# A two-block kernel: deferred norm and piecewise first loads in the retention layer, its q, k and out products as split passes, and the recurrent layer in thirds of its channels

## What is computed

```python
def rms_norm(x, g):
    y = x * rsqrt(mean(x * x, axis=-1) + 1e-6)
    return y * g

for layer in range(2):
    h = rms_norm(x, norm_g[layer, 0])
    m = retention_mixer(h, ret_w_in, ret_w_out) if layer == 0 else rglru_mixer(h, ...)
    x = x + rms_norm(m, norm_g[layer, 1])
    f = swiglu_ffn(rms_norm(x, norm_g[layer, 2]), ffn_w_in[layer], ffn_w_out[layer])
    x = x + rms_norm(f, norm_g[layer, 3])
```

```python
y, u = split(x @ w_in)                    # y = gelu(y), u = conv4(u)
r, i = sigmoid(u's blocks @ gate_w + gate_b)
log_a = -8 * r * softplus(-a_param); a = exp(log_a)
b = sqrt(-expm1(2 * log_a)) * (i * u)
h[t] = a[t] * h[t-1] + b[t]               # every channel by itself
out = (h * y) @ w_out
```

## Time and profile before

| what | value |
|---|---|
| median of 3 runs | 1721.5 us (1720.58 to 1722.06) |
| the profiled execution's own time | 1722.84 us |
| its span, first to last instruction | 1721.0 us |
| PE busy | 1590.1 us (92% of the span) |
| DVE, ACT, POOL busy | 678.4, 519.0, 40.8 us |
| chain that ended last | PE 80%, DVE 12%, ACT 5%, waiting for nothing shown 2% |
| moved by DMA | 382.88 MB, mean 222 GB/s |

### The profile page before, as it was taken

The page is one execution under the profiler, slowest core; times in us unless marked ns, Lnnn a source line. Parts: engine busy times, 40 slices in busy tenths (PEclk is TensorE's granted clock), DMA queues, the critical chain, the costliest instruction groups (busy, mean ns, idle before and its releaser), DMA issues.

```text
span 1721.0 us, 21762 instructions
## 1 busy us (share of the span) xinstructions
PE 1590.1 (92%) x9230; PEld 1179.3 (69%) x9230; DVE 678.4 (39%) x1059; ACT 519.0 (30%) x769; POOL 40.8 (2%) x37
## 2 busy tenths in 40 slices
PE   6999999999999599999889988787899999999996
PEld 6988689999898379999734675466444444444443
DVE  3433407665574617764334536602211121111112
ACT  5430025444454425444432214322111111011111
POOL 0000001000031001000000000000000000000000
PEclk8999999999999799999899999998899999999999
DMA  9543336455644445545621220020599999999991
GB/s 404 183 169 142 135 123 243 186 196 181 247 171 185 196 170 222 184 169 188 244 72 75 98 104 1 1 83 18 209 423 425 416 425 421 422 420 423 420 422 85
DMA packets 26985, 382.88 MB, mean 222 GB/s; under 512 B 3056, under 2 KB 3184, under 8 KB 3360
## 3 DMA queue, kind: packets, MB, share of 16 engines
q1 hardware_dynamic: 26208, 377.71, 55.5%
q0 software_dynamic: 704, 4.11, 0.6%
HBM read 380.76 MB, written 1.05 MB: 222 GB/s over the span
## 4 chain that ended last, share of the span: by engine, by line
PE 80%; DVE 12%; ACT 5%; issue 2%; DMA 1%; POOL 1%; DVEq 0%; ACTq 0%; SPq 0%; POOLq 0%
PE ps L478 71%; PE ps L876 4%; PE ps L885 4%; DVE w_lo L1268 2%; DVE HM L1280 2%; ACT HM L945 2%; DVE HM L1268 2%; DVE work L1280 2%; DVE work L1268 1%; ACT work L945 1%; ACT L945 1%; DVE X L1280 1%; DMA work<-in_ctx 1%; DVE work L1274 0%; DVE in_lo L1280 0%
## 5 line engine op out<-in xcount | busy, mean ns | idle before, releaser
L478 PE MATMUL ps<-ring,work 128*64 128x512 f32 x1536 | 336.9, 594 | 12.3 <-ACT work L945 12.3
L478 PE MATMUL ps<-in_hi,w_hi 128*128 128x256 f32 x896 | 255.9, 286 | 9.9 <-DVE in_lo L1280 5.1
L1268 DVE TENSOR_TENSOR w_lo<-ring,w_hi 128x1024 fp32r<-128x1024 f32 x156 | 200.4, 1291 | 158.9 <-ACT w_hi L945 158.9
L945 ACT ACTIVATE work<-ps 128x512 f32<-128x512 f32 (+2 forms) x148 | 87.3, 626 | 571.5 <-PE ps L478 324.2
L478 PEld LDWEIGHTS ps<-ring,work 128*64 128x64 f32 x1536 | 107.5, 137 | 222.0 <-issue 207.2
L478 PE MATMUL ps<-in_lo,w_hi 128*128 128x256 f32 x896 | 253.6, 283 | 0.0
L478 PE MATMUL ps<-in_hi,w_lo 128*128 128x256 f32 x896 | 253.5, 283 | 0.0
L945 ACT ACTIVATE w_hi<-ring 128x1024 fp32r<-128x1024 f32 x156 | 164.3, 1056 | 200.6 <-PE ps L478 159.4
L478 PE MATMUL ps<-HM,ring 128*128 128x256 f32 (+1 forms) x704 | 197.8, 441 | 6.8 <-ACT HM L945 6.8
L478 PE MATMUL ps<-work,ring 128*128 128x256 f32 x736 | 165.4, 388 | 18.8 <-DVE work L1268 18.8
L478 PEld LDWEIGHTS ps<-in_hi,w_hi 128*128 128x128 f32 x896 | 171.8, 192 | 15.0 <-issue 9.3
(11 more groups left out here) (192 smaller groups left out, 1704.6 us busy)
## 6 DMA issues: line engine op xcount, KB each, us to landing
ring<-in_experts SPq DMA_DIRECT2D x96, 2048.0 KB, 12.2
ring<-in_dense SPq DMA_DIRECT2D x83, 2048.0 KB, 8.1
cst<-in_ret_cst POOLq DMA_DIRECT2D x1, 1280.0 KB, 13.1
X<-in_x SPq DMA_DIRECT2D x1, 1024.0 KB, 5.8
cst<-in_ssd_cst POOLq DMA_DIRECT2D x1, 1024.0 KB, 4.9
work<-in_ctx POOLq DMA_DIRECT2D x1, 1024.0 KB, 8.6
out<-HM SPq DMA_DIRECT2D x1, 1024.0 KB, 3.8
cst<-in_wfour POOLq DMA_DIRECT2D x1, 256.0 KB, 2.8
```

The costliest lines, as they stand in the source:

```text
L478: i = pe.matmul(o, l, r, start=start, stop=stop)
L945: x = act.activation(o, i, f, **kw)
L1268: i = dve.tensor_tensor(out=o, in0=x, in1=y, op=op)
```

## The change

1. X is loaded in four pieces and the first weight unit in four, in the order x w x w x x w w (SP). POOL issues its table loads only when the four weight pieces have landed. The retention layer gets the deferred norm: ret_g's first 8 output blocks are made by `outer_gemm` from X times gain; the factor rstd is multiplied onto g by DVE (the Silu then works in place), onto v by ACT as a scale per token (rtok, which PE turns by two small matmuls and DVE copies), and onto q and k through the cosine and sine tables.
2. ret_q, ret_k and ret_out become split products. The gated output is split too: ACT writes its high part (gate_hi), DVE the low part in place (gate_lo). ret_out's first output block waits per head for gate_lo.
3. The dense stream turns through 5 slots of the ring; the sixth holds two of the three chunk buffer pairs (the third lies in H). Afterwards the expert units take all six slots, the sixth first.
4. In the recurrent layer each third (four channel blocks) goes through Exp, Tanh, Sqrt, scans and the gate product before the next third; lru_out is made third by third, for all 8 output blocks, from weights laid out by input block. The modulation strips 5 and 6 are read after the first third's Exp, strip 7 after its Tanh.
5. Renumbering of the norms and of semaphore counts that follows.

Buffers and slots:

```diff
+DENSE_SLOTS = 5
+SLOT = [u % DENSE_SLOTS for u in range(DENSE)]
...
+PART_SLOT = 5
+EXPERT_SLOT = [PART_SLOT] + [(DENSE + i) % DENSE_SLOTS for i in range(DENSE_SLOTS)]
...
-OUTER = ("ffn_in0", "lru_u", "ffn_in1")
+OUTER = ("ret_g", "ffn_in0", "lru_u", "ffn_in1")
...
-        w_at = [("cst", 0), ("HM", 0), ("work", 2 * KF * T)]
+        w_at = [("ring5", 0), ("ring5", 2 * CHUNK), ("HM", 0)]
...
+        sg_hi, sg_lo = over("work", 0, "sg_hi", KV, T), over("work", 8192, "sg_lo", KV, T)
```

SP, which issues the loads, and POOL:

```diff
-            sp.dma_start(X[:, :, :], a["x"]).then_inc(s["ld_x"], 16)
...
+            for j, piece in enumerate(("x", "w", "x", "w", "x", "x", "w", "w")):
+                if piece == "x":
+                    n = (0, None, 1, None, 2, 3)[j]
+                    sp.dma_start(X[:, 2 * n:2 * n + 2, :], a["x"][:, 2 * n:2 * n + 2, :]).then_inc(x_in[n], 16)
+                else:
+                    n = (None, 0, None, 1, None, None, 2, 3)[j]
+                    part = slice(n * CHUNK, (n + 1) * CHUNK)
+                    sp.dma_start(ring[0][:, part], a["dense"][0][:, part]).then_inc(first_in[n], 16)
+            for u in range(1, DENSE):
+                if TURN[u]:
+                    sp.wait_ge(slot_used[SLOT[u]], TURN[u])
...
+            sp.wait_ge(s["chunk_used"], CHUNKS)
+            for n in range(RING):
+                if EXPERT_SLOT[n] != PART_SLOT:
+                    sp.wait_ge(slot_used[EXPERT_SLOT[n]], DENSE_USES[EXPERT_SLOT[n]])
+                load_expert(n, n)
...
         def _(pool):
+            for j in range(4):
+                pool.wait_ge(first_in[j], 16)
```

PE:

```diff
-            norm_sums(squares_of_input(0))
-
-
-            split_gemm("ret_g", KV, KD, in_hi, in_lo, input_split(0), tile="g")
+            next_input(0, "ret_g", ())
+            split_gemm("ret_g", KV, KD, in_hi, in_lo, tile="g", first_m=BPC)
+            pe.wait_ge(s["rstd_ready"], 1)
+            for tau in range(2):
+                mm(ps[:, STAT, T + tau:T + tau + 1], rstd[:, tau * P:(tau + 1) * P], ones[:, 0:1], True, True,
+                   s["rtok_full"] if tau == 1 else None)
...
-            gemm("ret_q", "q", 8, KD, lambda c: H[:, c, :])
-            gemm("ret_k", "k", 8, KD, lambda c: H[:, c, :])
+            split_gemm("ret_q", KD, KD, in_hi, in_lo, tile="q")
+            split_gemm("ret_k", KD, KD, in_hi, in_lo, tile="k")
...
-            gemm("ret_out", "ret_out", KD, KV, lambda c: sg[:, c, :])
-            next_input(0, "ffn_in0", (1, 2))
+            split_gemm("ret_out", KD, KV, sg_hi, sg_lo, lambda c: pe.wait_ge(s["gate_lo"], 2 * (c // 4 + 1)))
+            next_input(1, "ffn_in0", (1, 2))
...
-            gemm("lru_out", "lru_out", KD, KL, lambda c: li[:, c, :], lambda c: pe.wait_ge(s["go_ready"], c // 4 + 1))
...
+            for n in range(3):
+                w = weights("lru_out", n)
+                pe.wait_ge(s["go_ready"], n + 1)
+                for b in range(4 * KD):
+                    c, m = (b // KD, b % KD) if n < 2 else (b % 4, b // 4)
```

ACT: the first input, the retention stage, and the recurrence, where Exp, Tanh and Sqrt now stand in one loop over n:

```diff
+                        fn(in_hi[:, c, :], X[:, c, :], ACT.Identity, s["in_hi_ready"], scale=col("norm_g", 2 * i * KD + c))
+                        if i == 0 and c == 2 * j and j < 3:
+                            weights_hi(j + 1)
...
+            for step, h in ((deviation, 0), (deviation, 1), (gate_hi, 0), (deviation, 2), (gate_hi, 1), (deviation, 3),
+                            (mod_read, 0), (gate_hi, 2), (gate_hi, 3)):
...
             for n in range(3):
-                mod_read(5 + n)
...
+                if n == 0:
+                    mod_read(5)
+                    mod_read(6)
                 act.wait_ge(s["a_ready"], n + 1)
...
-            for n in range(3):
+                if n == 0:
+                    mod_read(7)
                 act.wait_ge(s["lsq_arg"], n + 1)
```

DVE:

```diff
+            for j in range(8):
+                t = TILE["g", j]
+                weights_lo(chunks_by("ret_g", j))
+                dve.wait_ge(s["rstd_ready"], 1)
+                await_full(dve, t)
+                tt(sg[:, 2 * j:2 * j + 2, :], cut(bank(t), 2, T), rstd2, MUL, bank_read[t % ROT])
...
+            tt(cut(rcos, 2, T), cut(rcos, 2, T), rstd2, MUL)
+            settle(tt(cut(rsin, 2, T), cut(rsin, 2, T), rstd2, MUL))
...
+            def gate_lo(h):
+                for tau in range(2):
+                    t = TILE[f"t{h}", tau]
+                    dve.wait_ge(s["gate_hi"], 2 * h + tau + 1)
+                    hi, lo = (x[:, 4 * h:4 * h + 4, tau * P:(tau + 1) * P] for x in (sg_hi, sg_lo))
+                    tt(lo, sg[:, 4 * h:4 * h + 4, tau * P:(tau + 1) * P], hi.bitcast(F32), SUB, s["gate_lo"])
...
-                            (decayed, 3), (head_norm, 2), (gated, 1), (head_norm, 3), (gated, 2), (gated, 3)):
+                            (decayed, 3), (head_norm, 2), (gate_lo, 0), (gated, 1), (head_norm, 3), (gate_lo, 1), (gated, 2),
+                            (gate_lo, 2), (gated, 3), (gate_lo, 3)):
...
                 stt(four(uc, n), four(uc, n), 1.0, r_tiles(4 * n, 4), ADD, MUL, s["lsq_arg"])
-            for n in range(3):
                 dve.wait_ge(s["lsq_ready"], n + 1)
```

More of the change, by code:

```diff
@@ L263, in two_blocks @@
         omv = at(48, 8, 2, of=small)
+        rtok = small[:, 80:82]
         osd, ors = small[:, 64:72], small[:, 72:80]
@@ new lines, in _, with load_expert, expert_rest @@
+            for u in range(1, DENSE):
+                if TURN[u]:
+                    sp.wait_ge(slot_used[SLOT[u]], TURN[u])
+                sp.dma_start(ring[SLOT[u]][:, :], a["dense"][u]).then_inc(slot_full[SLOT[u]], 16)
+            def load_expert(n, unit):
+                i = EXPERT_SLOT[n]
+                sp.dma_start(ring[i][:, :], a["experts"][bass.ds(unit, 1)].rearrange("u p n -> (u p) n")).then_inc(
+                    slot_full[i], 16)
+            def expert_rest(done):
+                with sp.Fori(0, EXPERT_UNITS // RING - 1) as b:
+                    for n in range(RING):
+                        early = 2 if n >= RING - 2 else 1
+                        sp.wait_ge(slot_used[EXPERT_SLOT[n]], b + done + (DENSE_USES[EXPERT_SLOT[n]] + early))
+                        load_expert(n, b * RING + n + RING)
@@ L710, in _ @@
             mod_cols(7)
-            gemm("lru_out", "lru_out", KD, KL, lambda c: li[:, c, :], lambda c: pe.wait_ge(s["go_ready"], c // 4 + 1))
-            next_input(2, "ffn_in1", (8, 9))
+            for m in range(0, KD, 2):
+                await_room(pe, TILE["lru_out", m // 2])
+            for n in range(3):
[3 more added lines that the diff above has]
+                    c, m = (b // KD, b % KD) if n < 2 else (b % 4, b // 4)
+                    t = TILE["lru_out", m // 2]
+                    last = n == 2 and c == 3 and m % 2 == 1
+                    mm(bank(t)[:, m % 2 * T:(m % 2 + 1) * T], w[:, (c * KD + m) * P:(c * KD + m + 1) * P], li[:, 4 * n + c, :],
+                       n == 0 and c == 0 and m % 2 == 0, last, bank_full[t % ROT] if last else None)
+            next_input(3, "ffn_in1", (8, 9))
             ffn(1)
@@ L1036, in _ @@
             act.wait_ge(s["ld_vec"], 16)
+            next_input(0, "ret_g", ())
             act.wait_ge(s["csil_zero"], 1)
             fn(csil[:, :, 0:2], cut(col("c", 0, 2 * KD), KD, 2), ACT.Silu, s["csil_ready"])
[L1039 to L1044 removed]
             for j in range(8):
                 weights_hi(chunks_by("ret_g", j))
[L1047 removed]
+                await_read(act, TILE["g", j])
+                fn(pairs(sg, j), pairs(sg, j), ACT.Silu, s["g_ready"])
             for j in range(8):
```

229 lines of the change are left out of this document (124 added, 105 removed).

## The result

The change makes the kernel faster: 1680.0 us in the median of four runs (1678.56 to 1682.44) against 1721.8 (1720.58 to 1722.95). The ratio is 0.9761, 95% interval [0.9749, 0.9773]. The profiled execution took 1678.7 us, with a span of 1676.6. The forecast was 1678.6 within 1671 to 1694.

A forecast was written before the change was run, and what follows sets the result against it. PE was taken as the bound, busy 92% of the span, with DVE busiest from 169 to 194 us. From 1722.84, -12.0 + 0.6 - 9.4 - 9.4 - 12.7 = -42.9 gave 1679.9; the median, 1.3 lower, 1678.6, range 1671 to 1694.

The forecast's parts named there:

- The head: Start of the retention layer: PE's first pass at 8.0 us instead of 21.27, less 1.3 for stalls; -12.0 us.
- q and k: Retention layer's q and k products: eight split tiles at 5.73 us instead of 6.91, -9.4; two rtok matmuls +0.6 at most.
- at the 0.42 MB/us of a full queue that is 1.9 us, 5.6: Start of ret_g: the X and weights behind the first DMA take 1.9 us and have landed at 5.6 us.
- The price of 1.3 for stalls: In ret_g's 48 us, PE idle 1.3 us in all, scaled from ffn_in0; the ends were 0 and 5.
- ACT has about 1 us idle per chunk there, so nothing goes to PE: In ret_g, DVE's waits for ACT's small Exp and Ln between weight parts cost PE 0.
- before it paid that ramp at 21.3, now it pays it at 8, so I set no term: Start of ret_g: PE's half-clock start costs the same before and after the change, so 0.
- ret_out: Retention layer's output product: 128 split blocks save 9.4 us; its start unchanged, 0, with 5.4 as the other end.
- The recurrent layer: Recurrence and lru_out in thirds: PE starts earlier, then runs without waiting, ending at 619.4 instead of 632.15; gain 12.7 us.
- All this: 0: Dense slots, unit landing in lru_out and ffn_in1, and expert units at the experts' start: no change in time, 0.
- Pieces that pay each for itself: Rival in the head: small DMAs don't overlap, chunk 3 starts 10.4 us later, total 1689.0; chance 0.10.
- DVE and ACT as the pace in the retention layer: Rival: splits and rotary step don't fit in 5.73 us, ret_out waits for the last head; 13.4 us, 1692.0; chance 0.13.
- The expert stream: Rival in the experts: each pair waits for one unit more, 5.0 us x 16 pairs = 80, total 1758; chance 0.03.

## Why the prediction was right

**The head: -10.1 against -12.0.** (The two matmuls for rtok, +0.6, come after the last gate tile and are counted with q and k.) The mechanism held, and its start was mis-sized. The step "at the 0.42 MB/us of a full queue that is 1.9 us, 5.6" was the wrong one: that rate is from loads of 2 MB. The first weight piece was in hand at 7.03, not 5.6, because with the eight pieces the queue moved 223 GB/s from 3 to 6 us and 298 from 6 to 9; with one load each it moved 412 and 421. ACT's table load of 1.28, which the sum left out, stood behind X's landing, but the first input's high part was still done 0.21 us before the weight piece came, so it cost nothing. Start 9.44 for 8.0; other executions of the same code started up to 1.0 later.

The price of 1.3 for stalls was too small, and stood for other places. Successive passes show five gaps in ret_g of the changed kernel, 2.3 us in all: at 20.15 (0.43 more than a pass), at 26 for the two products of the tokens' sums (0.43), at 35.20 behind three table loads (0.27), at 44.38 (0.54) and 47.94 (0.60). The first stands behind a low part that took DVE 2.92 us instead of 1.22. POOL did the tokens' sums beside it (from 17.69 to about 25), and in eleven of the twelve profiled executions with the change the low part at this place took 2.40 to 2.93; so the prediction was right to look at POOL here, though not for a wait. Only two of them show a gap of PE behind it. The last two come from the step "ACT has about 1 us idle per chunk there, so nothing goes to PE": the idle time was there, but it was ahead of the Silu, with the next chunk's high part behind it. Both are gone with the Silu one tile later. Against the gaps stands a gain of 0.8 that was not foreseen: "before it paid that ramp at 21.3, now it pays it at 8, so I set no term" is not exact, as the ramp was 5.2 us long before (passes 0.21 apart from 21.27 to 26.5) and 3.6 us after (9.44 to 13.0). By what is told below of such starts, this gain is luck.

**q and k: -8.7 against -8.8** (9.4 less the 0.6 for rtok), and 9.5 for the split alone by the run without it. The pace was 5.7 a tile. The cover was there, as the run with two more products shows.

**ret_out: -10.1 against -9.4**, 10.4 by the run without it. The pace was foreseen; the half-clock stretch at its start was shorter (passes 0.21 apart for 2.4 us, of a cost of 1.2, where 1.9 was taken over). Its start moved by 0.3 in 24.8, where 0 was taken and 5.4 was the other end. The reading that PE does not wait for the last head was right: the last low part was written 4.2 us after the start.

**The recurrent layer: -13.0 against -12.7.** The first third was ready 14.7 after the last gate instead of 14.4, PE ran 43.5 instead of 44.0. Strip 7 came back as foreseen (DVE's last chain and Sqrt at 539.06). A table load is followed by the first activation after 1.30 us each time (530.58 to 531.88, 540.13 to 541.43). The further 1.38 us per switch that the Trainium skill gives ("ScalarE: Activation LUTs", What ACT_TABLE_LOAD costs) is in none of these rows; four more switches in this stretch cost nothing on the path.

**"All this: 0" was wrong twice, with opposite signs.** The new place of the chunk buffers gave 1.3 of the 1.4 us in each feed-forward net (shown by the run with the old places), and the experts took 3.0 more, where "29.9 as before" was forecast. The prediction had named a longer expert pair as a sign of being wrong, and on the experts it was. The ring and the units were looked at, what PE's queue does between the hidden values and the down product was not; the order of the waits there gives half of the loss back, the other half is unexplained. A further 2.6 ahead of the experts belongs to no part of the change: the norm's sums there, the same 16 passes, took 6.68 and 5.36 us before and 5.22 and 3.72 after. PE of the changed kernel:

```profile
801.92 5.22 PE L518 MATMUL ps<-SQ,ones 128*128 128x256 f32 x16 [2.62 <-ACT SQ L995]
809.95 3.72 PE L518 MATMUL ps<-SQ,ones 128*128 128x256 f32 x16 [2.81 <-ACT SQ L995]
```

These differ by execution: in the twelve profiled executions with the change they took 5.22 to 6.77 and 3.72 to 5.41 us, and the values of before lie in both ranges. So the total came out within 0.1%, but in part by luck, since the misses cancel: head +1.9, q and k +0.1, start of ret_out -0.3, ret_out -0.7, feed-forward nets -2.8, recurrent layer -0.1, ahead of the experts -2.6, experts +3.0. They add up to -1.5, which is the span's -44.4 against the forecast -42.9; sizes of up to 3 us stood in the single terms.

**The rivals.** Pieces that pay each for itself: no, the run with one load each is 3.5 slower in the head, and the last piece of the first unit was in use at 16.1 instead of 26.9. The rule of the Trainium skill to batch DMAs to 1 MiB or more ("DMA: Bandwidth & Descriptors", Bandwidth) would have been wrong by that here. What is true of it is that the queue moved about half while it worked on them (223 against 412 GB/s from 3 to 6 us); the first pass was earlier all the same, since it needs only the first two pieces. DVE and ACT as the pace in the retention layer: no, with 0.9 + 0.4 us idle on DVE in each tile. The expert stream: a pair did take longer, by 0.2 and not by 5.0; no unit was late.

## What to carry to other kernels

When a start is moved forward and its loads are cut into pieces, don't take the rate of large loads for them: the queue moved 223 GB/s with the pieces and 412 without. And follow both engines of a hand-off in their own order: idle time on an engine is cover only if the work that PE waits for isn't queued behind that idle time. Work in thirds pays when producer and consumer are both cut: with the consumer (PE) whole, all of the 13 us was lost, with the producer whole 6.9. A buffer at another place can change the pace of every pass that reads it (here by 0.8%); and in a loop of PE put the wait that comes last behind the others (0.10 us per turn here).

## What the runs showed of the hardware

A start of PE after standing idle has no fixed cost. The same first product of the layer ran its first 12, 15, 22 and 26 passes about 0.21 us apart, instead of 0.12, in four profiled executions (of the kernels with the weights first, the changed one, the Silu one later, and the separate semaphores): 1.1 to 2.4 us. The granted clock of the span goes with the time: 0.979 at 1675.0, 0.978 at 1678.7, 0.975 at 1682.1. Differences of one or two us between kernels can't be read from a median of five; they have to be read from the rows of a stage.

Right after the start the granted clock in the windows can't be trusted. Changed kernel:

```profile
9.40:11.00 1.60, 1.56 (x7) 1.59 (x8) 0.73 (x2) 0.72 (x1) 0.00 (x0) 1.00 1.04 416
...
174.40:176.90 2.50, 2.50 (x13) 2.50 (x12) 2.40 (x5) 1.23 (x2) 0.00 (x0) 0.50 1.00 288
```

Both stretches have passes 0.21 us apart (7 in 1.6, 13 in 2.5), the first after PE had done nothing at all and with a granted clock of 1.00, the second after short work and waits and with 0.50, the lower level of 1.2 GHz. In the first the pace of the passes tells it, not the column. The clock records of this trace begin at 13.10 us, where the passes become 0.12 apart, so the 1.00 ahead of them rests on no record.

The place of a chunk's buffers in memory sets the pace of split passes by 0.8% (170.52 against 169.2 us for a net), with the same instructions and PE full in both (422 against 419 passes in 50 us). Waits that PE's weight-load queue carries out ahead of a product cost 0.1 us per pair of experts when they stand behind the one that comes last.

A subtraction on DVE over 128x1024 elements that runs beside POOL's sums is longer: 2.92, 2.17, 2.31 and 1.66 us for the four from 17.18 us on in the changed kernel, against 1.22 to 1.23 for those before and after. What links the two was not tried.
